# Queries and ten merge gates of a hybrid decoder layer as seven-product block pairs ahead of the attention, with the turned probabilities' copy moved in front of the exponentials

## The reference

```python
h = rmsnorm(x, norm_mix_g)
proj = h @ w_in                       # 2048 x (1024 + 1536 + 48 + 1024 + 1024 + 4096)
q, kv, nsa_g, u, v, merge_g = split(proj)
kc, vc = compress_blocks(kv[0]), compress_blocks(kv[1])      # 31 compressed tokens per group
o_a = nsa_attention(q, kc, vc, kv[2], kv[3], kv[4], kv[5], sigmoid(nsa_g))
o_b = spatial_gating(gelu(u), gelu(v), ...)
g = sigmoid(merge_g).reshape(b, s, 2, 2048)
x = x + (g[0] * (o_a @ w_proj_a) + g[1] * (o_b @ w_proj_b)) @ w_mix_out
x = x + cross_attention(rmsnorm(x), rmsnorm(mem))
x = x + (silu(gate) * up) @ w_ffn_out                        # gate, up = rmsnorm(x) @ w_ffn_in
return rmsnorm(x, norm_final_g)
```

## Time and profile before

| | |
|---|---|
| median of 3 runs | 2777.14 us (2775.67 to 2778.92) |
| the profiled execution, first to last instruction | 2772.1 us |
| the difference of the two | 5.0 us |
| PE, PEld busy | 99%, 83% |
| DVE, ACT, POOL busy | 74%, 39%, 16% |
| granted clock of PE | 1.0 of full speed in all 40 slices |
| chain that ended last | PE 85%, DVE 6%, ACT 3%, DMA 2% |

### The profile page before, as it was taken

One profiled execution on the slowest core, in us unless ns is written; L12 is line 12 of the kernel. 1 busy time (PEld: TensorE's weight loads), 2 busy tenths in 40 slices (PEclk: granted clock), 3 DMA queues, 4 the chain that ended last, 5 costly groups with the idle time before them and its releaser, 6 DMA issues.

```text
span 2772.1 us, 37764 instructions
## 1 busy us (share of the span) xinstructions
PE 2737.9 (99%) x14015; PEld 2313.9 (83%) x14015; DVE 2050.9 (74%) x3133; ACT 1083.8 (39%) x1831; POOL 442.5 (16%) x406
## 2 busy tenths in 40 slices
PE   8999999999999999999999999999999999999998
PEld 7888788888888888888877888888888888788886
DVE  7544476776655555555678899999999999988887
ACT  6201254444420322211144555555555555443334
POOL 0200133343320445511000000000000000010000
PEclk9999999999999999999999999999999999999999
DMA  8532323322233444544334788888888888899882
GB/s 248 165 93 74 86 77 96 96 77 81 80 110 91 108 135 136 155 114 114 110 115 127 187 198 213 213 205 211 208 219 201 215 198 260 290 307 302 289 269 95
DMA packets 610806, 455.19 MB, mean 164 GB/s; under 512 B 13669, under 2 KB 555225, under 8 KB 604761
## 3 DMA queue, kind: packets, MB, share of 16 engines
q1 hardware_dynamic: 551328, 405.97, 49.3%
q0 software_dynamic: 46416, 30.41, 8.2%
q10 hardware_dynamic: 12904, 16.71, 1.9%
HBM read 394.06 MB, written 58.98 MB: 163 GB/s over the span
## 4 chain that ended last, share of the span: by engine, by line
PE 85%; DVE 6%; ACT 3%; issue 2%; DMA 2%; POOL 1%; ACTq 0%; DVEq 0%; SPq 0%; POOLq 0%
PE banks L893 12%; PE banks L894 12%; PE banks L895 12%; PE banks L1293 9%; PE banks L1290 9%; PE banks L1291 9%; PE banks L1355 4%; PE banks L1357 4%; PE banks L1356 4%; PE banks L1062 1%; PE banks L1121 1%; PE banks L1123 1%; PE banks L1122 1%; PE banks L1093 1%; PE banks L1078 1%
## 5 line engine op out<-in xcount | busy, mean ns | idle before, releaser
L1372 DVE CAST w_hi<-raw 128x512 fp32r<-128x512 f32 x424 | 229.1, 540 | 357.6 <-PE banks L895 292.7
L893 PE MATMUL banks<-act_hi,w_hi 128*128 128x512 f32 (+1 forms) x1232 | 489.3, 397 | 0.0
L894 PE MATMUL banks<-act_lo,w_hi 128*128 128x512 f32 (+1 forms) x1232 | 481.1, 390 | 0.0
L895 PE MATMUL banks<-act_hi,w_lo 128*128 128x512 f32 (+1 forms) x1232 | 481.0, 390 | 0.0
L1374 DVE TENSOR_TENSOR w_lo<-raw,w_hi 128x512 fp32r<-128x512 f32 x424 | 314.2, 741 | 14.6
L1291 PEld LDWEIGHTS banks<-t_hl,wf_lo 128*128 128x128 f32 x1312 | 246.5, 188 | 58.3
L895 PEld LDWEIGHTS banks<-act_hi,w_lo 128*128 128x128 f32 (+1 forms) x1232 | 230.2, 187 | 51.3
L893 PEld LDWEIGHTS banks<-act_hi,w_hi 128*128 128x128 f32 (+1 forms) x1232 | 230.7, 187 | 40.7 <-DVE w_lo L1374 0.6
L894 PEld LDWEIGHTS banks<-act_lo,w_hi 128*128 128x128 f32 (+1 forms) x1232 | 230.9, 187 | 39.4
L1293 PE MATMUL banks<-t_hl,wf_hi 128*128 128x512 f32 x656 | 259.4, 396 | 0.0
L1290 PE MATMUL banks<-t_hl,wf_hi 128*128 128x512 f32 x656 | 259.2, 395 | 0.0
(11 more groups left out here) (323 smaller groups left out, 5351.8 us busy)
## 6 DMA issues: line engine op xcount, KB each, us to landing
raw_f<-in_w_ffn_in_dram SPq DMA_DIRECT2D x82, 1024.0 KB, 8.9
raw<-in_w_in_dram SPq DMA_DIRECT2D x68, 1024.0 KB, 5.6
h_full<-hidden_blocks SPq DMA_DIRECT2D x35, 1024.0 KB, 8.1
wo_raw<-in_w_ffn_out_dram SPq DMA_DIRECT2D x32, 1024.0 KB, 10.1
hidden_blocks<-tok_hl SPq DMA_DIRECT2D x44, 512.0 KB, 6.2
s<-in_w_ffn_in_dram SPq DMA_DIRECT2D x40, 512.0 KB, 5.9
s<-in_w_ffn_in_dram POOLq DMA_DIRECT2D x40, 512.0 KB, 6.5
raw<-in_w_mix_out_dram SPq DMA_DIRECT2D x16, 1024.0 KB, 6.1
```

The costliest lines, as they stand in the source:

```text
L893: pe.matmul(dst, w_hi[:, q, j, 0:m], hi, start=first, stop=False)
L894: pe.matmul(dst, w_hi[:, q, j, 0:m], lo, start=False, stop=False)
L895: return pe.matmul(dst, w_lo[:, q, j, 0:m], hi, start=False, stop=last)
L1372: dve.tensor_copy(w_hi[:, q, :, 0:width], src).then_inc(hi_done, 1)
```

## The change

Of the 32 merge tiles, six (`m0`) are formed as plain tiles ahead of `c`, in the place right behind the memory's values. Behind them come nine pairs by seven block products: the eight query tiles and ten merge tiles. Their results go to DRAM (`queries`, `merge_gates`), and the queries are read back once into `q_t`. Sixteen merge tiles stay as the attention's filler. For the block form the sums of the activations' blocks are needed: DVE forms those of the high parts (`row_sums`), adds POOL's sums of the low parts (`row_sums_whole`) and, after ACT's high part, forms the low part (`row_sums_low`), all of it between the weight quarters of `m0`; there ACT makes the weights' high parts instead of DVE. `k` now stands ahead of the compression's hidden layer, and that layer's weights are loaded after the pairs. The queries are scaled when their high and low parts are made. In an attention step ACT copies the turned probabilities first and then forms the exponentials.

The diff, cut to its core (the joins have the form of the feed-forward part; they, the tiles' places and the semaphores' counts are left out):

```diff
@@ -37,6 +37,10 @@
+PLAIN_GATES = 6
+G_TILES = [("q", n) for n in range(0, 8, 2)] + [("merge", n) for n in range(PLAIN_GATES, PLAIN_GATES + 10, 2)]
+G_PAIRS = len(G_TILES)
+GATES_AHEAD = PLAIN_GATES + 10
@@ -175,8 +180,8 @@
-        ("mk", (4,)), ("mv", (4,)), ("c", (4,)), ("q", (8,)), ("k", (4,)), ("v", (4,)), ("g", (1,)),
-        ("merge", (32,)), ("sv", (8,)), ("su", (8,)), ("ab", (16, 4, 2, 2)), ("wo", (16,)),
+        ("mk", (4,)), ("mv", (4,)), ("m0", (PLAIN_GATES,)), ("c", (4,)), ("k", (4,)), ("v", (4,)), ("g", (1,)),
+        ("merge", (2 * DK - GATES_AHEAD,)), ("sv", (8,)), ("su", (8,)), ("ab", (16, 4, 2, 2)), ("wo", (16,)),
@@ -552,7 +584,7 @@
-        GATE_TILES = 32 * DK
+        GATE_TILES = PH["merge"].n * DK
@@ -684,16 +731,36 @@
+            for p in range(G_PAIRS):
+                if p == 0:
+                    sp.wait_ge(mem_kept, 32)
+                if p == 1:
+                    sp.wait_ge(split_done, PH["m0"].end())
+                if p >= 2:
+                    sp.wait_ge(g_lo, G_BASE + 7 * (p - 1))
...
+            sp.wait_ge(g_lo, G_BASE + 7 * (G_PAIRS - 1))
             columns(PH["c"], w_in_v, C_KV)
...
-            sp.wait_ge(turned, DK)
+            sp.wait_ge(g_unit, G_BASE + G_UNITS)
...
-            columns(PH["q"], w_in_v, C_Q)
+            sp.wait_ge(g_joined, g_join(J21, G_PAIRS - 1))
...
+            sp.wait_ge(g_stored, G_DMA0 + 32 * G_PAIRS)
+            sp.dma_start(q_t[:], q_dram.rearrange("(k p) t -> p k t", p=P)).then_inc(q_landed, 16)
@@ -975,16 +1042,55 @@
+            def half_unit(p, pos, dst, start, both):
+                g = 7 * p + pos
+                pe.wait_ge(g_lo, G_BASE + g + 1)
+                w_h, w_l = wg_hi[g % 3], wg_lo[g % 3]
+                for k in range(HK):
+                    last = k == HK - 1
+                    if k % 2 == 0:
+                        pe.matmul(dst, w_h[:, k], both(k), start=start and k == 0, stop=False, skip_group_check=True)
+                    mm = pe.matmul(dst[:, 0], w_l[:, k], both(k)[:, 0], start=False, stop=False, skip_group_check=True)
+                    if k % 2 == 1:
+                        mm = pe.matmul(dst, w_h[:, k], both(k), start=False, stop=last, skip_group_check=True)
+                mm.then_inc(g_unit, 1)
...
+            pe.wait_ge(mv_ready, 4)
+            for p in range(G_PAIRS):
+                bx, by, bz = (bank[2 * m + p % 2].rearrange("p (h t) -> p h t", h=2) for m in (1, 2, 3))
+                if p >= 2:
+                    pe.wait_ge(g_joined, g_join(J21, p - 2))
+                half_unit(p, 0, bx, True, row_block(0, 0))
+                if p == 0:
+                    pe.wait_ge(n_lo_done, N_LO0 + HK)
+                half_unit(p, 1, by, True, row_sum(0))
+                pe.wait_ge(g_kept, G_BASE + 3 * p + 1)
+                half_unit(p, 2, bx, False, row_sum(1))
+                half_unit(p, 3, bz, True, row_block(1, 0))
+                pe.wait_ge(g_kept, G_BASE + 3 * p + 3)
+                half_unit(p, 4, bx, False, row_sum(2))
+                pe.wait_ge(g_kept, G_BASE + 3 * p + 2)
+                half_unit(p, 5, by, False, row_block(1, 1))
+                pe.wait_ge(g_joined, g_join(J22, p))
+                half_unit(p, 6, bx, False, row_sum(3))
@@ -1435,14 +1541,108 @@
+            def row_sums(k):
+                a, b = act_hi[:, k].bitcast(F32), act_hi[:, HK + k].bitcast(F32)
+                t = n_sum[k]
+                dve.tensor_tensor(t[:, 0], a[:, 0:HT], a[:, HT:T], ALU.subtract).then_inc(n_summed, 1)
+                dve.tensor_tensor(t[:, 2], b[:, HT:T], a[:, HT:T], ALU.subtract).then_inc(n_summed, 1)
+                dve.wait_ge(n_summed, N_SUM0 + 5 * k + 1)
+                dve.tensor_tensor(t[:, 1], b[:, HT:T], t[:, 0], ALU.add).then_inc(n_summed, 1)
+                dve.wait_ge(n_summed, N_SUM0 + 5 * k + 3)
+                dve.tensor_tensor(t[:, 3], b[:, 0:HT], t[:, 1], ALU.subtract).then_inc(n_summed, 1)
+            def row_sums_whole(k):
+                dve.wait_ge(n_low_summed, N_LOW0 + 4 * k + 4)
+                dve.wait_ge(n_summed, N_SUM0 + 5 * k + 4)
+                dve.tensor_tensor(n_sum[k][:], n_sum[k][:], n_low[k % 2][:], ALU.add).then_inc(n_summed, 1)
+            def row_sums_low(k):
+                dve.wait_ge(n_hi_done, N_HI0 + k + 1)
+                dve.tensor_tensor(n_lo[k][:], n_sum[k][:], n_hi[k][:].bitcast(F32), ALU.subtract).then_inc(n_lo_done, 1)
...
+            for item in range(4, 4 * ph.n):
+                n, q = divmod(item, 4)
+                low(ph, *ph.at(n), q)
+                k = (item - 4) // 2
+                if item % 2 == 0 and k < HK:
+                    if k == 0:
+                        dve.wait_ge(quarters_done, PH["mv"].end())
+                    row_sums(k)
+                if item % 2 == 1 and k < HK:
+                    row_sums_whole(k)
+                if item % 2 == 0 and 0 < k <= HK:
+                    row_sums_low(k - 1)
@@ -1475,13 +1676,15 @@
+                        dve.scalar_tensor_tensor(out=q_hl[h * HD:(h + 1) * HD, hu % 2, e, 1], in0=q_t[rows, 2 * j + pr, qi * P:(qi + 1) * P],
+                                                 scalar=-HD ** -0.5, in1=q_hl[rows, hu % 2, e, 0].bitcast(F32),
+                                                 op0=ALU.mult, op1=ALU.subtract).then_inc(q_lo, 1)
@@ -2075,6 +2279,81 @@
+            for b in range(2):
+                act.wait_ge(gate_stored[b], 16 * PLAIN_GATES // 2)
...
+                ahead(0)
+                if p > 0:
+                    g_store(p - 1)
+                act.wait_ge(g_unit, G_BASE + 7 * p + 1)
+                if p >= 1:
+                    act.wait_ge(g_joined, g_join(JZ, p - 1))
+                act.activation(g_corners[:, 0], bx, ACT.Copy).then_inc(g_kept, 1)
@@ -2161,8 +2437,6 @@
-                if step < ITEMS:
-                    exps(step)
@@ -2173,6 +2447,8 @@
                         act.activation(prob_t[:, n % 2, 0, 0:cols_n], bank[4 + n % 2][:, 0:cols_n], ACT.Copy).then_inc(p_hi, 1)
+                if step < ITEMS:
+                    exps(step)
@@ -2478,21 +2749,37 @@
+            pool.wait_ge(turned_lo, DK)
+            for k in range(HK):
+                a, b = act_lo[:, k].bitcast(F32), act_lo[:, HK + k].bitcast(F32)
+                u = n_low[k % 2]
+                wait(pool, n_summed, 5 * (k - 1), N_SUM0)
+                pool.tensor_tensor(u[:, 0], a[:, 0:HT], a[:, HT:T], ALU.subtract).then_inc(n_low_summed, 1)
...
+                pool.wait_ge(g_s1_copied, G_DMA0 + 16 * p)
+                pool.dma_start(gs1[:].rearrange("p (k n) -> p k n", n=P), w_in_v[:, HK:DK, col:col + P], accum_op=ALU.add).then_inc(g_s1_added, 16)
```

More of the change, by code:

```diff
@@ L986, in _ @@
+            ph = PH["c"]
             runs(pe, ph.n // 2, plain)
+            ph = PH["k"]
+            for n in range(ph.n):
+                group(ph, *ph.at(n), hi16, lo16, low=2 * (n - 1))
+            pe.wait_ge(g_joined, g_join(J21, G_PAIRS - 1))
             pe.wait_ge(w1_landed, 32)
@@ L1468, in _ @@
             key_low(3)
+            split(ph, 0, 1)
             dve.wait_ge(cmp_hi, 1)
@@ new lines, in _ @@
+            ph = PH["m0"]
+            for item in range(4, 4 * ph.n):
+                n, q = divmod(item, 4)
+                high(ph, *ph.at(n), q)
+                k = (item - 4) // 2
+                if item % 2 == 0 and 0 < k <= HK:
+                    row_sums_high(k - 1)
+                if q == 1:
+                    gates_out(ph, n - 1, n - 1, gate_m0)
+            act.wait_ge(quarters_done, ph.end() - 2)
+            g_unit_high(0)
+            g_unit_high(1)
+            gates_out(ph, ph.n - 1, ph.n - 1, gate_m0)
```

296 lines of the change are left out of this document (233 added, 63 removed).

## The result

The changed kernel takes 2784.77 us (median of 7 runs, 2782.84 to 2787.12) against 2776.17 us of the kernel before on the same chip (7 runs): ratio 1.0033, 95% interval 1.0023 to 1.0042. It is slower by 8.6 us, 0.3%, where I had forecast 2768.5. The profiled span grew from 2772.1 to 2783.1 us.

A forecast was written before the change was run, and what follows sets the result against it. PE's queue was taken as the bound up to the end of the attention. Terms -20.3 + 2.5 + 1.0 + 0.5 + 7.6 = -8.7 gave a span of 2763.4 and 2768.5 us, range 2757 to 2781.

The forecast's parts named there:

- Products: Nine pairs of query and gate tiles go from 21.76 to 19.50 us each: -20.3 us.
- start of the pairs: Before the third unit's weights, ACT waits for the last plain gate to land in DRAM: +1.0 us, between 0 and 3.
- Row sums in the plain stage: Beside six plain tiles, DVE and POOL form activation sums; DVE needs 7.0 us per k-block, PE gives 5.44: +2.5 us.
- can begin about 77 ... DVE is there at 77 + 6 x 7.0 = 119: Plain stage: DVE starts about 77 us and reaches quarter 16 at 119, due on PE at 116.7.
- My bound of 12.5: Plain stage: upper bound of the row sums' cost if all eight DVE operations lengthen, 8.7 us each block.
- The rule of the Trainium skill: DVE and POOL share ports under an exclusive lock per instruction; plain stage 13.7 us late, sum 2779.7.
- Rival (3): Plain stage: DVE waits a whole POOL operation, 4 x 0.90 us per block, 13.7 us late; 2779.7, chance 0.12.
- Attention: With half its filler gone, PE waits for DVE: 3.8 us in the first query row, 3.8 later; +7.6, bounds 0 and 17.
- I take 0.16 us each, between 0 and 0.5: Attention: lateness of each of the other 24 pairs of heads after PE's lead absorbs most: 3.8 us.
- rival (4): Attention twice as late, each later pair of heads at its 0.5 us bound: 3.8 + 12, 2776.7 us; chance 0.10.
- Rival (2), waits stay,: Attention: three quarters of DVE's 119.3 us waits for ACT's turned copies stay, PE stands 48 us: 2809; chance 0.09.
- The 5.0 us around the span: Median of the runs, 2777.14, minus the profiled span, 2772.1; taken to lie around the span in both kernels.

The follow-up runs named there:

- The two runs that undo one cause each: Changed kernel with ACT's copy of the memory values later: 2778.88 us; changed kernel with whole sums on DVE and no POOL operations: 2777.41 us.
- the later weighing: Products with the turned probabilities two steps behind their turn, not one, against the changed kernel with whole sums on DVE and memory values' copy later: 2765.27 us.

## Why the prediction was wrong

*Products: right.* -20.3 us, units at 19.51 us per seven, no pause in their middle; key panels without a wait (forecast +0.5, the stretch was 1.3 us shorter); start of the pairs 1.6 where I had 1.0.

*Row sums in the plain stage: wrong, 2.5 forecast, 11.6 measured.* The price of a k-block, 7.0 us, was right to the hundredth. What failed is the step "can begin about 77 ... DVE is there at 77 + 6 x 7.0 = 119", twice. Ahead of DVE stood ACT's queue, with a copy that waits for PE's work behind its first tile; I had followed DVE's own queue only. DVE began at 86.3, and with the copy moved 5.3 us came back. And the sum takes the lateness at quarter 16, the first of its block, though the sums and the low part stand in front of the second. By the sum's own numbers DVE comes to quarter 17 at 119 + 5.3 and ends it 0.7 later, at 125.0, against 119.4 on PE: 5.6 late and not 2.5. The run with the copy moved lost 71.6 - 65.3 = 6.3 us. The two runs that undo one cause each took off 5.3 and 7.0 us, both together 11.3: the causes overlap by 1 us. My bound of 12.5 held the size, by another mechanism (all eight operations of a block lengthened), which didn't occur: four were.

*The rule of the Trainium skill* ("SBUF — State Buffer", section "SBUF: two separate sides"), a lock held for a whole instruction: a whole POOL operation in front of each of four DVE operations would have made a block 8.9 us; the rows show 7.00 and 7.10. They agree with taking turns, one DVE operation lengthened for each of POOL's, but a 128x256 operation of each together take 0.88 us (111.76 to 112.64), less than the 0.34 and 0.70 that they take from start to start alone. Rival (3) fell with its price, though the stage lost nearly its 13.7 us.

*Attention: wrong in size, 7.6 forecast, 17.5 measured, and in the first row wrong in mechanism too.* The first row lost 5.1 (forecast 3.8), and that these are close is luck: I had put it down to DVE's 5.6 us of work against PE's 4.96, but DVE was busy 39.27 of 45.80 us, 86% and not over 90, and with the later weighing the row took 42.0 us with DVE's work unchanged. For the 24 later pairs of heads the failed step is "I take 0.16 us each, between 0 and 0.5": they lost 12.3 / 24 = 0.51 each, the upper bound. That is the size of rival (4), which with 15.8 us had 10%. I had let PE's lead of 1.5 us "take most of the lateness up"; but PE and its weight loads stood 15 and 21 times for `prob_t`, up to 1.4 and 1.8 us, and the run with the later weighing, which widens just this lead, got 7.1 us back. For the other 10.5 us the cause stays open; PE waits then for POOL's scaled probabilities. How much is lost depends on the filler: 17.6 us with sixteen tiles, 4.4 with twenty, none with twenty-four.

*Rival (2), waits stay,* did not occur, since the new order removed them; undone, it gave 2847 where I had reckoned 2809: nearly all of the waits came back, 111.1 of 119.3 us, and not three quarters. Had only the plain term failed, the time would have been 2778; had only the attention failed, 2778 too: it took both to leave my range.

*The 5.0 us around the span* that the prediction adds were a wrong reading. In each later run an execution is only 1.7 to 1.9 us longer than its own span (2784.81 against 2783.1), so the profiled execution of the kernel before was a quick one. In spans the forecast was 2763.4 and the measured 2783.1: the terms missed by 19.7 us, and 3.3 of them are hidden in the time.
